# Hybrid decoder trunk on one core: norm inputs turned in halves, cross queries computed transposed, two bank pairs in the feed-forward, expert tokens fetched by an indirect transfer

## The reference

```python
# even layer (0)
u = rmsnorm(x, g0) @ w_in_ab
x = x + concat(pool_mixer(u_pool), moba_attention(q, k, v)) @ w_out_ab    # 12 heads of 64
x = x + cross(rmsnorm(x, g1))                                            # 4 heads, memory of 256 tokens
x = x + swiglu(rmsnorm(x, g2))                                           # width 2816
# odd layer (1)
x = x + nsa_mixer(rmsnorm(x, g3)) @ w_out_c                               # 16 heads, three branches
x = x + cross(rmsnorm(x, g4))
h = rmsnorm(x, g5)
p = softmax over the top 2 of 8 router logits h @ router_w
x = x + sum over the 2 chosen experts e: p[e] * ((silu(h @ wg[e]) * (h @ wu[e])) @ wd[e])   # width 3584
return rmsnorm(x, final_g)
```

## Time and profile before

| | us |
|---|---|
| median of 3 runs | 1684.62 (1684.47 to 1685.3) |
| the profiled execution | 1684.51 |
| its span | 1682.8 |
| PE busy | 1589.7 |
| DVE busy | 1250.4 |
| ACT busy | 1077.1 |
| POOL busy | 23.4 |
| mean granted clock of PE | 0.961 |

### The profile page before, as it was taken

The page is one execution under the profiler, slowest core; times in us unless marked ns, Lnnn a source line. Parts: engine busy times, 40 slices in busy tenths (PEclk is TensorE's granted clock), DMA queues, the critical chain, the costliest instruction groups (busy, mean ns, idle before and its releaser), DMA issues.

```text
span 1682.8 us, 21706 instructions
## 1 busy us (share of the span) xinstructions
PE 1589.7 (94%) x7714; PEld 1317.2 (78%) x7715; DVE 1250.4 (74%) x1354; ACT 1077.1 (64%) x1276; POOL 23.4 (1%) x52
## 2 busy tenths in 40 slices
PE   6988789998999976999999999999999999999997
PEld 5767678886888766788888888888888888888885
DVE  4545345555524743898998998998998998998996
ACT  4454344444425451787877877877877877877874
POOL 5000000000000000000000000000000000000000
PEclk9999799999968996999999999999999999999999
DMA  9510244666421142799999999999999999999960
GB/s 359 202 46 0 76 150 158 217 226 237 166 101 51 35 141 100 255 388 357 357 359 344 370 360 346 363 364 339 376 359 337 376 353 343 371 361 342 365 247 25
DMA packets 199808, 434.15 MB, mean 258 GB/s; under 512 B 6906, under 2 KB 35668, under 8 KB 199764
## 3 DMA queue, kind: packets, MB, share of 16 engines
q1 hardware_dynamic: 197184, 432.22, 71.1%
q0 software_dynamic: 288, 1.05, 0.2%
q10 hardware_dynamic: 2292, 0.28, 0.1%
HBM read 432.49 MB, written 1.05 MB: 258 GB/s over the span
## 4 chain that ended last, share of the span: by engine, by line
PE 91%; DVE 4%; ACT 3%; issue 1%; ACTq 1%; DVEq 0%
PE ps L1145 18%; PE ps L1150 18%; PE ps L1147 18%; PE ps L637 8%; PE ps L640 7%; PE ps L643 7%; PE ps L768 3%; PE ps L1116 2%; PE ps L1171 1%; PE ps L709 1%; PE ps L733 1%; DVE f_w_lo L1631 1%; PE ps L951 1%; ACT f_w_hi L1249 1%; DVE hT_lo L1643 1%
## 5 line engine op out<-in xcount | busy, mean ns | idle before, releaser
L2140 DVE TENSOR_TENSOR w_lo<-ring,w_hi 128x1024 fp32r<-128x1024 f32 x672 | 813.5, 1224 | 55.7 <-ACT w_hi L1556 15.7
L1556 ACT ACTIVATE w_hi<-ring 128x1024 fp32r<-128x1024 f32 x672 | 712.3, 1062 | 185.0 <-PE ps L1150 185.0
L1145 PE MATMUL ps<-w_hi,x_hi 128*128 128x512 f32 x896 | 354.0, 395 | 2.4 <-DVE x_lo L2146 2.4
L1147 PE MATMUL ps<-w_hi,x_lo 128*128 128x512 f32 x896 | 350.0, 391 | 0.0
L1631 DVE TENSOR_TENSOR f_w_lo<-ring,f_w_hi 128x1024 fp32r<-128x1024 f32 (+1 forms) x139 | 169.0, 1225 | 145.3 <-ACT f_w_hi L1249 144.9
L1150 PE MATMUL ps<-w_lo,x_hi 128*128 128x512 f32 x896 | 276.6, 390 | 0.0
L1249 ACT ACTIVATE f_w_hi<-ring 128x1024 fp32r<-128x1024 f32 (+1 forms) x139 | 145.1, 1056 | 163.6 <-PE ps L643 155.1
L637 PE MATMUL ps<-f_w_hi,hT_hi 128*128 128x512 f32 (+2 forms) x480 | 187.2, 394 | 19.9 <-DVE hT_lo L1643 10.3
L1145 PEld LDWEIGHTS ps<-w_hi,x_hi 128*128 128x128 f32 x896 | 168.7, 188 | 36.8 <-issue 2.6
L1150 PEld LDWEIGHTS ps<-w_lo,x_hi 128*128 128x128 f32 x896 | 168.5, 188 | 36.3
L1147 PEld LDWEIGHTS ps<-w_hi,x_lo 128*128 128x128 f32 x896 | 168.8, 188 | 34.1
(11 more groups left out here) (250 smaller groups left out, 1284.9 us busy)
## 6 DMA issues: line engine op xcount, KB each, us to landing
ring<-in_moe_w_gate SPq DMA_DIRECT2D x56, 2048.0 KB, 8.5
ring<-in_moe_w_up SPq DMA_DIRECT2D x56, 2048.0 KB, 9.1
ring<-in_moe_w_down SPq DMA_DIRECT2D x56, 2048.0 KB, 8.2
...
```

The source lines that it names most:

```text
L1145: pe.matmul(ps[:, bnk, :], hi, w_h, start=first_ and (bnk != part.open), stop=False, skip_group_check=True)
L1147: pe.matmul(ps[:, bnk, :], lo, w_h, start=False, stop=False, skip_group_check=True)
L1556: sc_.activation(w_hi[:, high_e.k % STAGES, :], raw(slot, q), ACT.Copy).then_inc(hi_ready, 1)
L2140: ve.tensor_tensor(w_lo[:, st, :], raw(slot, q), w_hi[:, st, :].bitcast(F32), ALU.subtract).then_inc(lo_ready, 1)
```

## The change

- **Halves.** `turn_in` becomes `turn_half`: 8 transposes for half of the width, into banks 4 and 5, put on PE inside the stage before (after a part, or between the high and the low products of a part). The squares are halved too, and the root adds the halves through its bias.
- **Cross queries** are computed transposed (`turned_q`: weights as the left operand), so that the second turn falls away; the token's factor moves into the scale of the exponential and into `tops`. The keys' turns move to the K/V product and into MoBA. The turn of the result goes by token tile, and the output product goes column half by column half (`by_columns`).
- **Feed-forward.** Even and odd steps use banks 6, 7 and 4, 5; the order becomes down(s) with the turn of step s + 1 inside, then gate_up(s + 2). The last step goes by columns.
- **Pooling** uses banks 6 and 7 of its own, its second product moves behind MoBA's first turns.
- **Start.** The first load comes in four pieces with a semaphore each, ACT's first table is loaded early, evictions and splits alternate, and six small loads move behind them in ACT's queue.
- **Experts.** POOL stores `h` to HBM. In step 5 of a round PE multiplies `sel` by the token numbers (`find_rows`), DVE makes integers of the result, POOL fetches those rows (`fetch`), and in step 6 PE turns them with 8 transposes (`turn_rows`). The first gather stays.

```diff
+    def first_load():
+        kind, w, at, n = HEAD_UNITS[0]
+        for q in range(PARTS):
+            sp.dma_start(slot_cols(0, n)[:, 2 * q:2 * q + 2, :],
+                         cols(w, at, n)[:, 2 * q:2 * q + 2, :]).then_inc(first_weights[q], 16)
+        t.next(weights_used)
...
+    def fetch():
+        pool.wait_ge(row_of_ready, t.next(row_of_ready))
+        pool.sem_inc(rows_asked, 1)
+        pool.indirect_dma_start(rows_in, None, token_rows[:, :], bass.IndirectOffsetOnAxis(ap=row_of[:, 0:1], axis=0)).then_inc(rows_landed, 16)
+    pool.wait_ge(h_ready, 1)
+    pool.dma_start(token_rows.rearrange("(t p) d -> p t d", p=P), h[:, :, :]).then_inc(rows_stored, 16)
+    pool.wait_ge(rows_stored, 16)
+    pool.wait_ge(routed, 1)
+    n_more = pool.value_load(rounds[0:1, 0:1], min_val=NE - 1, max_val=2 * NE - 1)
+    fetch()
+    with t.loop(pool, 0, n_more, {row_of_ready: 1}) as it:
+        fetch()
...
+    def turn_half(of, half, stands=None, follows=True):
+        if stands is not None:
+            stands()
+        if follows:
+            turned_stand()
+        clear()
+        for j in range(2):
+            for n in range(2):
+                for tt in range(TT):
+                    k = 4 * half + 2 * j + n
+                    mm = pe.transpose(ps[:, 4 + j, (n * TT + tt) * P:(n * TT + tt + 1) * P],
+                                      of[:, tt, k * P:(k + 1) * P], ident[:, :])
+            mm.then_inc(xT_full, 1)
+            t.next(xT_full)
+    def x_before():
+        for tt in range(TT):
+            pe.wait_ge(acc_free[tt], acc.n[tt] - 1)
...
+    def turned_q(fresh):
+        b = [acc(pr) for pr in range(2)]
+        for q in range(2):
+            pe.wait_ge(f_hi_ready, t.next(f_lo_ready))
+            st = split_part.k % F_STAGES
+            split_part.k += 1
+            for k in range(4 * q, 4 * q + 4):
+                if k % 2 == 0:
+                    pe.wait_ge(hT_lo_ready, fresh + k // 2 + 1)
+                for pr in range(2):
+                    w = f_w_hi[:, st, (k % 4) * 256 + pr * P:(k % 4) * 256 + (pr + 1) * P]
+                    one = pe.matmul(ps[:, b[pr], 0:S], w, hT_hi[:, k, :], start=(k == 0), stop=False, skip_group_check=True)
+                    if k == pr == 0:
+                        one.then_inc(weights_used, 1)
+                    pe.matmul(ps[:, b[pr], 0:S], w, hT_lo[:, k, :], start=False, stop=False, skip_group_check=True)
+            if q == 0:
+                turn_half(xs, 1, x_before)
+            pe.wait_ge(f_lo_ready, t.value(f_lo_ready))
+            for pr in range(2):
+                for k in range(4 * q, 4 * q + 4):
+                    mm = pe.matmul(ps[:, b[pr], 0:S], f_w_lo[:, st, (k % 4) * 256 + pr * P:(k % 4) * 256 + (pr + 1) * P],
+                                   hT_hi[:, k, :], start=False, stop=(k == KD - 1), skip_group_check=True)
+                if q == 1 and pr == 0:
+                    mm.then_inc(acc_full[0], 1)
...
+    def by_columns(hi_of, lo_of, bank_of, full, start, needs=None, insert=None):
...
+        for c in range(2):
+            b = [bank_of(tt, c) for tt in range(TT)]
...
+                if c == tt == 1 and insert is not None:
+                    insert()
...
+                    w_h = f_w_hi[:, st[k], c * 512:(c + 1) * 512]
+                    one = pe.matmul(ps[:, b[tt], :], hi_of(k, tt), w_h, start=start and k == 0, stop=False, skip_group_check=True)
...
+                    pe.matmul(ps[:, b[tt], :], lo_of(k, tt), w_h, start=False, stop=False, skip_group_check=True)
+                    mm = pe.matmul(ps[:, b[tt], :], hi_of(k, tt), f_w_lo[:, st[k], c * 512:(c + 1) * 512], start=False,
+                                   stop=(k == 1), skip_group_check=True)
...
+    def cross(layer, fresh):
+        turned_q(fresh)
         x_stands()
-        turn_in(xs, KD)
-        project(256, True)
-        x_stands()
-        act_turn(pairs_of((0, P)))
-        pe.wait_ge(act_turn_done, t.value(act_turn_full))
         a = scores.k
-        scores(lambda par, j: x_qT[half_of(par), j, :], lambda par, j: x_kT[half_of(par), j, :], False)
+        scores(lambda par, j: x_qT[half_of(par), j, :], lambda par, j: x_kT[layer][half_of(par), j, :], False)
         turn_probs(a, x_probs, False)
         weighted(a, x_pT, lambda par, j, kc: kvm_v[:, layer, kc, 2 * j + par, :], False)
...
+        y = t.value(xT_full)
+        for tt in range(TT):
+            pe.wait_ge(heads_ready, t.next(heads_ready))
+            pe.wait_ge(act_turn_done, t.value(act_turn_full))
+            pe.wait_ge(dve_turn_done, t.value(dve_turn_full))
+            for n in range(2):
+                mm = pe.transpose(ps[:, 4 + tt, n * P:(n + 1) * P], u[:, tt, n * P:(n + 1) * P], ident[:, :])
+            mm.then_inc(xT_full, 1)
+            t.next(xT_full)
+        at = [slice(tt * P, (tt + 1) * P) for tt in range(TT)]
+        by_columns(lambda k, tt: hT_hi[:, 6 + k, at[tt]], lambda k, tt: hT_lo[:, 6 + k, at[tt]], lambda tt, c: acc(tt),
+                   acc_full, True, lambda tt: pe.wait_ge(hT_lo_ready, y + tt + 1), lambda: turn_half(xs, 0, x_before))
...
+    def down(s):
+        act_stands()
         for kc in range(2):
-            at = [slice((kc * TT + tt) * P, (kc * TT + tt + 1) * P) for tt in range(TT)]
-            split_part([(ps[:, 2 * tt + c, :], aT_hi[:, at[tt]], aT_lo[:, at[tt]], c * 512, 512, False,
-                         stop and kc == 1) for tt in range(TT) for c in range(2)],
+            split_part([(ps[:, 2 * tt + c, :], of_act(aT_hi, s, kc, tt), of_act(aT_lo, s, kc, tt), c * 512, 512, False,
+                         False) for tt in range(TT) for c in range(2)],
...
+            if kc == 0:
+                turn_act(s + 1)
+    def x_added(n):
+        return lambda: pe.wait_ge(ffn_added, n)
...
+    gate_up(0, range(PARTS), fresh, lambda: turn_half(xs, 1, x_stands))
+    for b in range(4):
+        pe.matmul(ps[:, b, 0:2], zeros[:, 0:DH].bitcast(BF16), zeros[:, 0:1].bitcast(BF16), start=True, stop=False,
+                  skip_group_check=True)
+    gate_up(1, (0,))
+    turn_act(0)
+    gate_up(1, (1, 2, 3))
+    with t.loop(pe, 0, (FSTEPS - 3) // 2, {f_lo_ready: 12, f_part_used: 12, act_ready: 4, turned: 2}) as i:
+        for s in range(2):
+            down(s)
+            gate_up(s + 2, range(PARTS))
+    down(FSTEPS - 3)
+    gate_up(FSTEPS - 1, range(PARTS))
+    down(FSTEPS - 2)
+    act_stands()
+    fresh = t.value(xT_full)
+    by_columns(lambda k, tt: of_act(aT_hi, FSTEPS - 1, k, tt), lambda k, tt: of_act(aT_lo, FSTEPS - 1, k, tt),
+               lambda tt, c: 2 * tt + c, down_full, False, None, lambda: turn_half(xs, 0, x_added(2)))
...
+        if half:
+            turn_half(xs, 1, x_stands, False)
+        for j in range(2):
+            pe.wait_ge(rT_ready[j], half + 1)
+        for tt in range(TT):
+            for k in range(4 * half, 4 * half + 4):
+                mm = pe.matmul(ps[:, b, tt * NE:(tt + 1) * NE], hT[:, k, tt * P:(tt + 1) * P], rw[:, k, :],
+                               start=(tt == k == 0), stop=(k == KD - 1), skip_group_check=True)
+                if tt == k == 0:
+                    mm.then_inc(weights_used, 1)
...
+    def find_rows():
+        pe.wait_ge(sel_ready, t.next(sel_ready))
+        for tt in range(TT):
+            mm = pe.matmul(ps[:, 7, S:S + 1], sel[:, tt, :], token[:, tt:tt + 1], start=(tt == 0), stop=(tt == TT - 1))
+        mm.then_inc(row_of_full, 1)
+    def turn_rows():
+        pe.wait_ge(rows_landed, t.next(rows_landed, 16))
+        for k in range(KD):
+            mm = pe.transpose(ps[:, 2 + k // 4, (k % 4) * P:(k % 4 + 1) * P], rows_in[:, k * P:(k + 1) * P], ident[:, :])
...
-                gather()
+                turn_rows()
...
+            if s == LAST - 1:
+                find_rows()
...
+    def squares(c, of=xs, into=ss):
+        if c:
+            sc_.wait_ge(squared, t.value(squared))
+        for tt in range(TT):
+            half = of[:, tt, c * 512:(c + 1) * 512]
+            sc_.activation(half if of is mem_x else junk[tt], half, ACT.Square, scale=D ** -0.5,
+                           accum_out=into[:, c, tt:tt + 1]).then_inc(squared, 1)
+            t.next(squared)
+        if c == 0:
+            sc_.wait_ge(squared, t.value(squared))
+            step(sc_.activation(into[:, 0, :], into[:, 0, :], ACT.Identity, bias=eps[:, 0:1]))
+    def root(of=ss):
+        sc_.wait_ge(squared, t.value(squared))
+        for tt in range(TT):
+            ins = sc_.activation(rms[:, tt:tt + 1], of[:, 1, tt:tt + 1], ACT.Sqrt, bias=of[:, 0, tt:tt + 1])
+        ins.then_inc(rms_ready, 1)
...
+    def cross(layer, slot, then=None):
         arrived(slot)
         high(slot, 0)
+        turn_half(3 * layer + 1, 0)
+        squares(0)
         high(slot, 1)
-        turn_in(3 * layer + 1)
-        square(0)
...
+        t.next(acc_full[0], 2)
+        turn_half(3 * layer + 1, 1)
+        squares(1)
+        root()
+        c = t.next(acc_full[0])
```

(45 more changed lines are left out.)

653 lines of the change are left out of this document (353 added, 300 removed).

## The result

The kernel became faster. The median of 4 runs is 1619.68 us (1611.41, 1612.71, 1626.65, 1627.79) against 1684.64 us; the ratio is 0.9613, 95% interval 0.955 to 0.9677. The profiled execution took 1611.41 us with a span of 1609.7 us.

A forecast was written before the change was run, and what follows sets the result against it. PE's queue was taken as the bound nearly everywhere, busy in 94% of the span. Terms 16.7 + 3.0 + 9.4 + 13.3 + 2.1 + 0 = 44.5 us took 1684.5 to 1640.0 us, range 1625 to 1663.

The forecast's parts named there:

- the term for the start: Kernel start: earlier first product, but six transfers issued from ACT's queue delay the fourth part; 0 us, bounds -1.5 and +3.5.
- the cross-attentions' group: From the projection's last part to the second step's gate_up (cross-attention, entry, first silu): 11.0 us gained.
- the prediction's own good bounds: Whole kernel: the favourable bounds of all terms together are 67.4 us, giving 1617 us.
- Experts: Expert rounds: fetch and eight transposes replace eight gathers, 2.09 us each, 16.7 us together; bounds 13.2 and 18.9.
- Cross-attentions: Both cross-attentions: shorter way to the scores, weighted product and turn of the result; 4.7 us each, 9.4 together, bounds 3 and 20.
- The chain ahead of the scores: Cross-attention: ACT's Exp load and split, then DVE's subtraction and copy of q, hold the scores; only 0.9 us gained.
- Last step and turn into layer C: End of the feed-forward: 1.5 us from the last step and 5.5 from the turn into the middle.
- Memory and K turns: Memory turn, pooling and K turns: shorter waits around the K/V product, less ACT's two evictions; 3.0 us, bounds 1 and 5.
- A late fetch: Rival in the experts: the fetch lands late, each us late costs 8 us; chance 0.20.
- The fetch as the bound: Rival in the experts: a fetch over 14.0 us makes the kernel slower than before, 1701 at 16 us; chance 0.07.
- the transfers' rate: Rival in the experts: 357 GB/s is the limit, an expert takes 124.7 us and the kernel 1668; chance 0.03.
- waits that eat the trunk's gains: Rival before the experts: waits in ACT's queue lose half of 27.8 us, giving 1654; chance 0.15.

The follow-up runs named there:

- b_nsa: The kernel before with 16 products of zeros on PE between layer C's last projection and the turns that follow; 1678.64 us median.
- a_cross: The changed kernel with products of zeros in each cross-attention, 16 ahead of the scores, 6 behind them, 3 behind the turns of the probabilities; 1605.09 us.
- a_late2: The changed kernel with 110 one-column memsets on POOL between its wait for the row numbers and the fetch; 1627.42 us median.

## Why the prediction was right and wrong

- **The first failed step is what the sum left out: layer C's attention.** The prediction took it at today's length and gave it neither a term nor a bound, though the kernel before stands at half clock there for 31 us. In some two of five runs of either kernel the time is 14 to 16 us shorter, and in the profiles of such runs that stretch is 3.5 to 7 us long and the stage 13.8 us shorter. The kernel before was read as if it had one time, since its runs agreed within 0.05%; that they all fell on one level was chance.
- **The second is the term for the start: 0 forecast with a bound of 3.5, 6.2 measured.** It set the 7.0 us of six issues between the pairs and the fourth part, and so counted a queue's issues as time of its engine. They cost 2.3 us, and the fourth part was split at 19.77 us, not at 26.5. The first product, forecast at 12.8, came at 12.00.
- **Neither alone puts the median out of the range.** It is the middle of two runs on each level, so layer C is worth about 7 of the 13.8 us in it: 1640 - 7 = 1633. With the start 1627, and the cross-attentions' group, 3.9 us over its forecast, takes it below 1625. On equal levels the gain is 57.6 us (1682.8 to 1625.2) by profiles and 58 to 59 by the runs, against 44.5, so the upper level of the changed kernel, 1627, lies inside the range, at its low end. The range itself stopped two thirds of the way to the prediction's own good bounds, 1617; all of them together would have held the median.
- **Experts: right.** 2.14 us per round for 2.09, the fetch at 7.6 to 7.9 us for 7 to 8.1, a few tenths of spare for 0.3. The rest of the 17.8 us is within what the clock at the stage's start makes (the kernel before took 1010.5 us there in `b_nsa`).
- **Cross-attentions: the mechanism right, the size low.** The chain ahead of the scores came as written, 0.5 to 0.9 us early per link. With entry and first silu the first one won 14.9 us for 11.0: 5.8 for 4.7 in the cross-attention itself, 4.2 for 2.8 in the entry, 4.9 for 3.5 in the silu. In the entry the wait of 1.0 us that the sum charged did not come; PE goes from the output product to gate_up with no gap. The silu is 3.2 us of idle and the half clock behind it, which the sum priced at 0.3. The row that it cites for this stands elsewhere, at 415.64, but the trace has the same 0.63 us per record behind the silu. The second cross-attention won 6.6 us and the router 0.9 for 2.1, 7.5 for 6.8 together. The upper bound of 20 for both, meant for a clock that stays up, was too low: to the 12.4 us of the change `a_cross`, with the clock at 0.96 and 1.00, adds 11.9.
- **Inside the first cross-attention errors cancel.** The chain won 1.9 us for 0.9, since its links came early, and the turn of the result 2.0 for 1.7. From the scores to the weighted product it was 0.6 for 2.1, since the scores took 3.78 us instead of 2.00. The output product won 1.3, which has no term: less of it ran at half clock.
- **Last step and turn into layer C:** 8.0 for 7.0. **Memory and K turns:** 3.7 for 3.0. **Steady steps:** 0.8 us of 160 where nothing was forecast; not followed up.
- **The rivals.** A late fetch is real and costs its lateness, shown by `a_late2`; in the changed kernel it came to 0.5 us. The fetch as the bound, the transfers' rate and waits that eat the trunk's gains did not occur. That the feed-forward part and the halves hide what they hide is read from the stages alone; no run took them apart.
